# Router weights in their own place in SBUF, and a turned shift-and-scale vector read back by one transfer

## The reference, cut to what matters

```python
def hybrid_layer(x, c, ...):
    mod = (jax.nn.silu(c) @ ada_w + ada_b)[:, None, :]
    sh1, sc1, gt1, sh2, sc2, gt2 = jnp.split(mod, 6, axis=-1)
    h = rmsnorm(x, norm1_g) * (1.0 + sc1) + sh1
    (aq, ak, av, ..., cg, ga, gb, gc) = split_cols(h @ w_in)
    o_a, o_b, o_c = dsa_attention(...), hgrn2(...), retention(...)
    merged = (sigmoid(ga) * (o_a @ w_branch_a) + sigmoid(gb) * (o_b @ w_branch_b)
              + sigmoid(gc) * (o_c @ w_branch_c))
    x = x + gt1 * (merged @ w_out)
    h2 = rmsnorm(x, norm2_g) * (1.0 + sc2) + sh2
    return x + gt2 * hier_moe(h2, rg_w, rg_b, re_w, re_b, e_gate, e_up, e_down)

def hier_moe(h, ...):   # 32 experts in 4 groups, 2 of the best group's 8 for each token
    group_logits = x @ rg_w + rg_b          # [256, 4]
    exp_logits = x @ re_w + re_b            # [256, 32]
    ...
    y = y + einsum(silu(x @ wg) * (x @ wu) * gates, wd)

def reference(...):
    return second_block(first_block(...), ...)   # dense FFNs, spatial gating, attention
```

## Time and profile before

| | |
|---|---|
| median of three runs | 2058.64 us (2057.87 to 2059.55) |
| the profiled execution | 2058.48 us, of which the span of instructions is 2056.6 us |
| TensorE busy | 1909.1 us, 93% |
| VectorE busy | 1129.6 us, 55% |
| ScalarE busy | 903.8 us, 44% |
| GpSimd busy | 126.4 us, 6% |
| DMA | 503.51 MB, mean 245 GB/s over the span |
| TensorE's granted clock | 0.971 of full speed on average |

### The profile page before, as it was taken

How to read it: one execution, slowest core, us unless ns; L and a number is a source line. 1 busy time by engine, 2 the same in 40 slices (tenths; PEclk the granted TensorE clock), 3 DMA queues, 4 the chain that set the end, 5 groups by cost and what they waited for, 6 DMA issues and landing times.

```text
span 2056.6 us, 30557 instructions
## 1 busy us (share of the span) xinstructions
PE 1909.1 (93%) x12776; PEld 1488.0 (72%) x12776; DVE 1129.6 (55%) x1523; ACT 903.8 (44%) x1288; POOL 126.4 (6%) x101
## 2 busy tenths in 40 slices
PE   9999999999999866766699999999999999999998
PEld 7899988889984311111178888888888888988887
DVE  3778874577662101001156666756666766756666
ACT  4655555554342100000045546645546555675554
POOL 0244331001110000000000000000000000000000
PEclk9999999999999978788999999999999999999999
DMA  9654545677999999999985655555555555524552
GB/s 351 207 167 145 164 148 168 207 255 242 353 382 416 425 425 424 426 426 425 420 311 184 236 188 185 179 164 165 190 193 169 184 186 191 174 90 168 191 184 83
DMA packets 243905, 503.51 MB, mean 245 GB/s; under 512 B 13617, under 2 KB 167858, under 8 KB 224562
## 3 DMA queue, kind: packets, MB, share of 16 engines
q1 hardware_dynamic: 242864, 500.70, 67.4%
q10 hardware_dynamic: 898, 0.80, 0.1%
HBM read 500.07 MB, written 1.07 MB: 244 GB/s over the span
## 4 chain that ended last, share of the span: by engine, by line
PE 72%; DMA 15%; DVE 7%; ACT 3%; issue 2%; SPq 1%; POOL 0%; ACTq 0%; DVEq 0%
PE bank L706 13%; PE bank L645 13%; PE bank L647 13%; PE bank L646 13%; PE bank L708 7%; DMA m<-in_expert_w_up 4%; DMA m<-in_expert_w_gate 4%; DMA m<-in_expert_w_down 4%; PE bank L1094 4%; DVE m L2269 2%; PE bank L1105 2%; DMA m<-in_ada_b 1%; ACT m L1570 1%; PE bank L975 1%; SPq L3361 1%
## 5 line engine op out<-in xcount | busy, mean ns | idle before, releaser
L2269 DVE TENSOR_TENSOR m<-m,m 128x1024 fp32r<-128x1024 f32 x505 | 623.0, 1248 | 282.3 <-ACT m L1570 280.3
L645 PE MATMUL bank<-m,m 128*128 128x256 f32 (+1 forms) x1960 | 661.5, 338 | 9.1 <-DVE m L2269 5.5
L647 PE MATMUL bank<-m,m 128*128 128x256 f32 (+1 forms) x1960 | 646.9, 330 | 0.0
L646 PE MATMUL bank<-m,m 128*128 128x256 f32 (+1 forms) x1960 | 646.3, 330 | 0.0
L1570 ACT ACTIVATE m<-m 128x1024 fp32r<-128x1024 f32 x505 | 523.8, 1054 | 230.1 <-PE bank L647 207.7
L706 PE MATMUL bank<-m,m 128*128 128x512 f32 x1248 | 439.8, 394 | 0.0
L645 PEld LDWEIGHTS bank<-m,m 128*128 128x128 f32 x1960 | 369.7, 189 | 59.0 <-DVE m L2269 12.7
L647 PEld LDWEIGHTS bank<-m,m 128*128 128x128 f32 x1960 | 369.5, 189 | 36.6
L646 PEld LDWEIGHTS bank<-m,m 128*128 128x128 f32 x1960 | 370.0, 189 | 35.1 <-issue 2.4
L708 PE MATMUL bank<-m,m 128*128 128x256 f32 x1248 | 352.7, 283 | 0.0
L706 PEld LDWEIGHTS bank<-m,m 128*128 128x128 f32 x1248 | 234.4, 188 | 54.0
(11 more groups left out here) (349 smaller groups left out, 1389.6 us busy)
## 6 DMA issues: line engine op xcount, KB each, us to landing
m<-in_ffn_w_in SPq DMA_DIRECT2D x88, 1024.0 KB, 5.1
m<-in_w_in SPq DMA_DIRECT2D x60, 1024.0 KB, 5.2
m<-in_ffn_w_out SPq DMA_DIRECT2D x44, 1024.0 KB, 4.9
m<-in_expert_w_up SPq DMA_DIRECT2D x40, 1024.0 KB, 20.5
m<-in_expert_w_down SPq DMA_DIRECT2D x34, 1024.0 KB, 16.4
m<-in_expert_w_gate SPq DMA_DIRECT2D x33, 1024.0 KB, 22.9
m<-in_expert_w_gate SPq DMA_DIRECT2D x15, 2048.0 KB, 23.5
m<-in_expert_w_down SPq DMA_DIRECT2D x13, 2048.0 KB, 18.4
```

The lines of the kernel that those rows point to most:

```text
L645: e.matmul(o, s[0], m[0], start=first, stop=False, skip_group_check=skip)
L646: e.matmul(o, s[0], m[1], start=False, stop=False, skip_group_check=skip)
L647: return e.matmul(o, s[1], m[0], start=False, stop=last, skip_group_check=skip)
L2269: inc(e.tensor_tensor(rv(fit(q.L, q.view.shape)), q.view, fit(q.H, q.view.shape), ALU.subtract), "l", skey(q, "L"))
```

## The change

It does six things. The router weights `rW` and `rB` get words 55360 to 55683, inside `ex 10`, in place of words inside `oc`. `router_in` moves from step 1 of branch B to step 1 of branch A. `ex 10` is loaded behind step 3 of branch C, after a wait for `rbias`, in place of step 1 of branch B. TensorE gets a transpose of `cols[:, 16:32]` behind the last `ada` sum of `cg3`, for which it waits for `("cols", 6)` to `("cols", 9)`; ScalarE copies the 16 x 128 result to `colt` (words 55232 to 55359). The write to the scratch tensor becomes one of `colt`, 16 rows of 512 bytes, behind step 0 of branch B. The 16 reads of single elements become one read of 128 x 2 rows of 32 bytes behind step 1 of branch B.

```diff
+        colt = mem(55232, 128)[0:16]
...
-        rW, rWg, rWs = [mem(o, 288).rearrange("p (k n) -> p k n", n=36) for o in (50736, 21504, 21792)]
-        rB = mem(51024, 36)
+        rW, rWg, rWs = [mem(o, 288).rearrange("p (k n) -> p k n", n=36) for o in (55360, 21504, 21792)]
+        rB = mem(55648, 36)
...
+            def channels_turned():
+
+                b = take("s", "colt")
+                for g in range(6, 10):
+                    w.wait_ge("cols", g)
+                full(e.transpose(b[0:16, 0:128], cols[:, 16:32], K(C_ID)), "colt")
...
             for g in range(4):
                 gemm1(f"cg{g}", hT, h_ready)
                 ada(*later[4 + g])
+                if g == 3:
+                    channels_turned()
             ticks.join()
...
+            b = got("colt")
+            taken(e.activation(colt, b[0:16, 0:128], ACT.Copy), "colt", also=[("colt",)])
             ticks.join()
...
                     g, q = adas[name][i]
                     run(("ada", g, q))
+                    if name == "A" and i == 1:
+                        router_in()
                     if g in (4, 10) and q:
                         ...
+                    if name == "B" and i == 0:
+                        w.wait_ge("colt")
+                        then_inc(e.dma_start(scr.ap()[0:2048].rearrange("(r n) -> r n", n=128), colt), "scr_out", ("colq",), by=16)
                     if name == "B" and i < 2:
-                        fetch(first("ex", 9 + i))
-                    if name == "B" and i == 1:
-                        w.wait_ge("full", ("ocT", 7))
-                        router_in()
-                        w.wait_ge("aM")
-                        for g in range(6, 10):
-                            w.wait_ge("cols", g)
-                        then_inc(e.dma_start(bass.AP(tensor=scr, offset=0, ap=[[16, 128], [1, 16]]), cols[:, 16:32]),
-                                 "scr_out", ("colq",), by=16)
-                    if name == "B" and i == 2:
-                        w.wait_ge("colq")
-                        for c in range(8):
-                            for z in range(2):
-                                src = bass.AP(tensor=scr, offset=8 * z + c, ap=[[128, 16], [16, 8]])
-                                then_inc(e.dma_start(colp[16 * c:16 * c + 16, 8 * z:8 * z + 8], src, allow_slow_non_contiguous=True),
-                                         "skew_in", ("colp",), by=16)
+                        if i:
+                            w.wait_ge("colq")
+                            then_inc(e.dma_start(colp.rearrange("p (z k) -> p z k", z=2),
+                                                 scr.ap()[0:2048].rearrange("(z p k) -> p z k", z=2, k=8)), "skew_in", ("colp",),
+                                     by=16)
+                        if i == 0:
+                            fetch(first("ex", 9))
...
+                        if i == 3:
+                            w.wait_ge("taken", ("rbias",))
+                            fetch(first("ex", 10))
```

## The result

The changed kernel takes 2062.92 us (median of 12 runs, 2061.8 to 2064.34) against 2058.69 us before (12 runs, 2057.07 to 2060.91). The ratio is 1.002, with a 95% interval of 1.0012 to 1.0027: slower by 0.1 to 0.3%. Forecast were 2063.3 us and a range of 2060.0 to 2067.0. The profiled execution took 2063.03 us.

A forecast was written before the change was run, and what follows sets the result against it. TensorE was taken to bound the branches and the time after the experts, DMA the stretch from 590 to 1035 us. Terms 4.4 + 1.6 − 3.8 + 2.5 = +4.7 us gave 2063.3 us, range 2060.0 to 2067.0.

The forecast's parts named there:

- The wait for the columns: Before branch B, TensorE's new transpose waits for VectorE's columns signal, delaying the first matmul: +4.4 us (4.2 to 4.7).
- The clock behind it: At the start of branch B, matmuls after the new 4 us hole run at a lower clock: +1.6 us.
- The `gt2` wait: In branch C, VectorE's wait for the late `gt2` bias and TensorE's resulting hole go: −3.8 us.
- two blocks of SyncE's queue: In branch B, issuing router loads and 16 reads takes together 23 us, holding back ring loads that could go.
- `ex 10` behind branch C: Its 1 MiB load moves into the full DMA stage, ahead of all later expert loads: +2.5 us.
- `router_in` in branch A and ScalarE's copy: Router loads fit among branch A's issues, and ScalarE's copy before branch B loses only what TensorE loses: nothing.
- kept `gt2` wait: Rival, chance 0.14: branch C's backlog has another source, so the 3.8 us stay: +8.5 us, 2067.1 us.
- The rival on the faster side: Rival, chance 0.07: the freed queue uses 8.1 us of idle DMA between 492.5 and 515: −3.4 us, 2055.2 us.

The follow-up runs named there:

- late turn: Changed kernel with TensorE's transpose of the columns and ScalarE's copy moved behind the first gate product of branch B: 2056.69 us, ratio 0.999 to before.
- columns half: Kernel before plus the columns' transpose (behind branch B's first gate product), one write and one read; router loads and `ex 10` as before: 2054.46 us, ratio 0.9978.
- router half: Kernel before with `rW` and `rB` inside `ex 10`, `router_in` in branch A, `ex 10` behind step 3 of branch C; columns as before: 2056.78 us, ratio 0.9992.
- wait alone: Kernel before plus only the columns' transpose behind `cg3`, copied to a place nobody reads: 2063.44 us, ratio 1.0023.
- `ex 10` alone: Kernel before with one load moved: `ex 10` behind step 3 of branch C, after `rbias`: 2057.43 us, ratio 0.9993.
- bias early: Kernel before with one load moved: the `gt2` bias behind step 2 of branch B instead of step 1 of branch C: 2055.38 us, ratio 0.9985.

## Why the prediction was right, and where not

*The wait for the columns, +4.4.* Right: 4.4, with the transpose and its releaser where they were placed. Taken away by the late turn, it takes its clock term with it, 6.2 us by the medians.

*The clock behind it, +1.6.* Right in kind, 2.4 in the profile shown, 1.2 and 1.0 behind the same hole in two other kernels. The bounds, nothing and 3.3, were the better statement than the value. The Trainium skill (TensorE: Matmul & The Clock Gate, What's actually happening) has the monitor that sets the clock run free of the kernel, so that its phase against a hole changes between executions. These profiles fit that, with 1.65 us and none behind two holes of 2.00 and 2.17 us, but nothing in them shows the monitor.

*The `gt2` wait, −3.8.* The size was right, −3.9 in the profile, and that the wait goes. The cause was told too narrowly. I put it on the two blocks of SyncE's queue. Two separate edits of the change are each enough, the columns half and the MiB of `ex 10` out of branch B, and so is the router half, which holds the second; whether the router's loads have a part of their own was not tested. The run with the wait alone shows that a later TensorE doesn't remove it. The step that failed is the one that priced `ex 10` in branch B at nothing ("where the engines had room"): with its MiB gone the router's issues and the 16 reads are shorter, the other loads are ahead, and the wait falls by 2.2 us. The edits don't add, since the wait costs nothing below a limit. By the starts of the matmuls VectorE could wait for 8.81 − 2.15 = 6.66 us before TensorE ran dry, and in the run with the wait alone for 8.99 − 2.33, 6.66 again; 6.58 us (router half, `ex 10` alone), 4.64 (columns half) and 4.23 (the change) are all under it.

*`ex 10` behind branch C, +2.5.* Right: +2.3 in the changed kernel, 2.3 in the run that moves it alone, 2.1 with the late turn and in the router half, and −0.4 to −0.2 in the expert stage in the runs where it stays early. Alone it makes a faster kernel all the same, by the term above.

*`router_in` in branch A and ScalarE's copy, nothing.* Right as far as the lateness shows: −0.16 us at 457 us in the changed kernel.

The sum was +4.7 and the profile has −0.2 + 4.4 + 2.4 − 0.4 − 3.9 − 0.1 + 2.3 = +4.5 (4.6 unrounded). The difference of the medians is 4.2. That it came this close is in part luck, as the clock term alone moves between 1.0 and 2.4 us. The stated range ends at 2067.0, 0.1 short of the 2067.1 of the kept `gt2` wait that it is said to take in. The rival on the faster side, by which the idle DMA time of branch B would be worth 8 us, is out: the queue ran empty again at 580 us.

## What to carry to other kernels

Ask of each wait that an edit adds when its signal is given in the trace, and not how small the work behind it is: a transpose of 0.3 us cost 6 to 7 us here because its input was due 4 us after the place where it was put, and 6 us further down it was free.

A load that is moved has two prices. In the stage that is bound by DMA here it cost its bytes, 2.1 to 2.3 us for 1 MiB; in a stage that isn't, it costs only if it makes something else land too late, and there the question is how much later that other load could land at no cost. So three different edits (the columns half, `ex 10` late, the bias early) can each be credited with the same gain, and only runs of each alone show that it is one and the same 3.8 us. The cheapest edit is to move the late load itself.

## What the runs showed of the hardware that was not expected

Holes of TensorE of nearly the same length were followed by different stretches at the lower clock: 4.1 us by 2.4 us of loss in one profile and by 1.2 and 1.0 in two others, 2.00 us by 1.65 and 2.17 us by nothing. A gain or loss of a microsecond or two behind a hole is not told by one profile.

The issue of a DMA on SyncE's queue took longer here when more was queued ahead of it: the same bias load took 3.69, 1.83 and 0.58 us to issue, and the same 16 reads 13.33 and 10.86 us.

Sixteen and twelve filler matmuls ahead of the wait went with a stand of TensorE of 3.3 to 4.2 us some 175 us later, in the expert stage, with no releaser in the profile; with 32 there was none. It wasn't settled.
